# Gated convolution layer on one core: the sixth output product's weight difference on VectorE, eight block sums in a row, and additions moved between them

## The reference

```python
hn = rms_norm(x, norm_g)
a, b, gate = split(hn @ w_in, 3)              # w_in 1024 x 3072
u = a * sigmoid(b)
u = causal_depthwise_conv(u, conv_w, 31 taps) + conv_b
u = silu(layer_norm(u, ln_g, ln_b)) * silu(gate)
y = x + u @ w_out                             # w_out 1024 x 1024
```

## Time and profile before

| | |
|---|---|
| median of three executions | 354.58 us (354.42 to 354.72) |
| the profiled execution's own time | 354.64 us |
| its span in the profile | 352.8 us |
| PE busy | 348.5 us, 99% of the span |
| DVE busy | 322.4 us, 91% |
| POOL busy | 267.0 us, 76% |
| ACT busy | 232.0 us, 66% |
| DMA over the span | 123 GB/s on average |

### The profile page before, as it was taken

One profiled execution on the slowest core, in us unless ns is written; L12 is line 12 of the kernel. 1 busy time (PEld: TensorE's weight loads), 2 busy tenths in 40 slices (PEclk: granted clock), 3 DMA queues, 4 the chain that ended last, 5 costly groups with the idle time before them and its releaser, 6 DMA issues.

```text
span 352.8 us, 4758 instructions
## 1 busy us (share of the span) xinstructions
PE 348.5 (99%) x1564; PEld 289.6 (82%) x1564; DVE 322.4 (91%) x516; ACT 232.0 (66%) x334; POOL 267.0 (76%) x192
## 2 busy tenths in 40 slices
PE   8999999999999999999999999999999999999996
PEld 8888888888888888888888888888888888878785
DVE  5679799999999999989999998998599999999972
ACT  6889685667936870998669777975784872443400
POOL 0119999999999999789999999895596551359240
PEclk9999999999999999999999999999999999999999
DMA  8995111201410321404110410441643498047152
GB/s 265 411 412 212 39 59 59 88 34 61 118 61 16 88 78 59 119 2 119 59 60 3 119 59 15 107 119 61 215 143 120 130 394 313 0 151 224 45 208 90
DMA packets 30520, 43.51 MB, mean 123 GB/s; under 512 B 18336, under 2 KB 18848, under 8 KB 30496
## 3 DMA queue, kind: packets, MB, share of 16 engines
q1 hardware_dynamic: 30352, 43.21, 36.5%
q10 hardware_dynamic: 144, 0.00, 0.0%
HBM read 34.82 MB, written 4.19 MB: 111 GB/s over the span
## 4 chain that ended last, share of the span: by engine, by line
PE 92%; DVE 5%; issue 1%; ACT 0%; DVEq 0%; ACTq 0%
PE mm L634 68%; PE acc L710 9%; PE mm L651 6%; PE mm L710 6%; DVE sgate L1254 2%; DVE nat L1266 2%; DVE x_lo L1234 1%; PE acc L756 1%; PE acc L691 1%; PE acc L701 1%; PE acc L628 0%; ACT x_hi L948 0%; PE acc L622 0%; PE acc L624 0%; DVE ones L1069 0%
## 5 line engine op out<-in xcount | busy, mean ns | idle before, releaser
L634 PE MATMUL mm<-x_hi,w_hi 128*128 128x512 f32 x352 | 137.4, 390 | 0.0
L634 PE MATMUL mm<-x_hi,w_lo 128*128 128x512 f32 x352 | 137.0, 389 | 0.0
L634 PE MATMUL mm<-x_lo,w_hi 128*128 128x512 f32 x352 | 137.0, 389 | 0.0
L1178 DVE SCALAR_TENSOR_TENSOR acc<-u,chan,acc 128x512 f32<-128x512 f32 x157 | 110.5, 748 | 0.1
L1484 POOL TENSOR_TENSOR pconv<-pconv,prod 128x512 f32<-128x512 f32 x60 | 78.4, 1349 | 1.3 <-ACT prod L865 1.3
L634 PEld LDWEIGHTS mm<-x_hi,w_lo 128*128 128x128 f32 x352 | 66.1, 188 | 13.8
L634 PEld LDWEIGHTS mm<-x_lo,w_hi 128*128 128x128 f32 x352 | 66.1, 188 | 13.6
L634 PEld LDWEIGHTS mm<-x_hi,w_hi 128*128 128x128 f32 x352 | 66.1, 188 | 13.4
L1178 DVE SCALAR_TENSOR_TENSOR acc<-u,w_sum,acc 128x512 f32<-128x512 f32 x90 | 67.2, 747 | 2.5 <-ACT acc L847 2.3
L865 ACT ACTIVATE prod<-u,chan 128x512 f32<-128x512 f32 x69 | 47.9, 716 | 19.9 <-POOL pconv L1484 18.5
L1428 POOL TENSOR_TENSOR w_lo<-raw,w_hi 128x1024 fp32r<-128x1024 f32 (+1 forms) x21 | 50.3, 2395 | 8.7 <-ACT w_hi L814 8.6
(11 more groups left out here) (109 smaller groups left out, 527.6 us busy)
## 6 DMA issues: line engine op xcount, KB each, us to landing
raw<-w_in SPq DMA_DIRECT2D x22, 512.0 KB, 3.3
nat<-x_t SPq DMA_DIRECT2D x16, 256.0 KB, 5.4
sgate<-x SPq DMA_DIRECT2D x8, 512.0 KB, 10.2
raw<-w_out SPq DMA_DIRECT2D x8, 512.0 KB, 3.3
nat<-x SPq DMA_DIRECT2D x8, 512.0 KB, 7.7
y<-nat SPq DMA_DIRECT2D x15, 256.0 KB, 2.2
raw_late<-w_out SPq DMA_DIRECT2D x4, 512.0 KB, 4.3
sig<-w_out SPq DMA_DIRECT2D x4, 512.0 KB, 4.1
```

Source lines behind the costliest of these rows:

```text
L634: ins = nc.tensor.matmul(bank(("unit", m, h)), w[:, m % 3, k, :], xx[:, k, half(h)], start=(k == 0 and i == 0), stop=(k == KC - 1 and i == 2))
L1178: ins = nc.vector.scalar_tensor_tensor(dst, chain_in(j, chain, k), tap(j, chain, k), chain_bank(j, chain), ALU.mult, ALU.add)
```

## The change

The weight difference of b = 5 goes from POOL to DVE (`less_11`), and with it the semaphore that ACT and SP wait for. On DVE the sums of 5 and of 4 now stand in a row with no additions to the output between them, and additions that stood before and between them are spread behind. POOL's low halves of b = 4 wait for the last of the sums of 4, where they waited for the last of 5; its low halves of b = 5 wait for the last low part of v of b = 5 (6 x 4 of them), where the difference waited for the last of b = 4 (5 x 4).

```diff
-         ("12-11", 5, 0), ("12-11", 5, 1), ("lo", 5, 0), ("lo", 5, 1), ("lo", 6, 0), ("lo", 6, 1)]
+         ("lo", 5, 0), ("lo", 5, 1), ("lo", 6, 0), ("lo", 6, 1)]
-W_BY_VECTOR = {("+11", 4, 0): 1, ("+11", 4, 1): 2, ("lo", 3, 0): 3, ("lo", 3, 1): 4}
+W_BY_VECTOR = {("+11", 4, 0): 1, ("+11", 4, 1): 2, ("lo", 3, 0): 3, ("lo", 3, 1): 4, ("12-11", 5, 0): 5, ("12-11", 5, 1): 6}
-W_PAUSES = {("22-12", 2, 0): CK, ("lo", 2, 0): 2 * CK, ("21-", 3, 0): 4 * CK, ("12-11", 5, 0): 5 * CK, ("lo", 6, 0): 7 * CK}
+W_PAUSES = {("22-12", 2, 0): CK, ("lo", 2, 0): 2 * CK, ("21-", 3, 0): 4 * CK, ("lo", 5, 0): 6 * CK, ("lo", 6, 0): 7 * CK}
...
             for i in range(2):
-                sp.wait_ge(wb_done, W_OP["12-11", 5, i])
+                sp.wait_ge(wb_late, W_BY_VECTOR["12-11", 5, i])
                 load_w_out("a", i, 1, 1)
...
-                elif b == 4:
-                    act.wait_ge(wb_late, W_BY_VECTOR["+11", 4, i])
+                elif b in (4, 5):
+                    act.wait_ge(wb_late, W_BY_VECTOR[{4: "+11", 5: "12-11"}[b], b, i])
...
+            def less_11(i):
+
+                dve.wait_ge(wo_in[1][i], 64)
+                dve.wait_ge(wo_in[0][i], 48)
+                nc.vector.tensor_tensor(w_source(5, i), w_source(5, i), w_raw("a", i), ALU.subtract).then_inc(wb_late, 1)
...
             posts(2, (0,))
             for i in range(2):
                 finish_wb_lo(3, i)
-            posts(2, (1,))
+            posts(2, (1, 2))
             for k in range(CK):
                 sum_v(5, k)
-            posts(2, (2, 3))
             for k in range(CK):
                 sum_v(4, k)
+            posts(2, (3,))
+            posts(3, (0, 1))
             for k in range(CK):
                 split_v(4, k)
-            posts(3)
+            for i in range(2):
+                less_11(i)
+            for k in range(CK):
+                split_v(5, k)
+            posts(3, (2, 3))
             posts(4, (0, 1))
-            for k in range(CK):
-                split_v(5, k)
             for k in range(CK):
                 sum_v(6, k)
...
                 if op == ("lo", 4, 0):
-                    pool.wait_ge(vsum_ready, vsum_count(5, CK - 1))
+                    pool.wait_ge(vsum_ready, vsum_count(4, CK - 1))
```

More of the change, by code:

```diff
@@ L873, in split_w_out @@
                     act.wait_ge(wo_in[0][i], 16 if b == 1 else 64)
-                elif b == 4:
-                    act.wait_ge(wb_late, W_BY_VECTOR["+11", 4, i])
+                elif b in (4, 5):
+                    act.wait_ge(wb_late, W_BY_VECTOR[{4: "+11", 5: "12-11"}[b], b, i])
                 else:
-                    act.wait_ge(wb_done, W_OP[{2: "22-12", 3: "21-", 5: "12-11"}[b], b, i])
+                    act.wait_ge(wb_done, W_OP[{2: "22-12", 3: "21-"}[b], b, i])
                 if b == 3:
@@ L1370, in _ @@
                 finish_wb_lo(3, i)
-            posts(2, (1,))
+            posts(2, (1, 2))
             for k in range(CK):
                 sum_v(5, k)
-            posts(2, (2, 3))
             for k in range(CK):
                 sum_v(4, k)
+            posts(2, (3,))
+            posts(3, (0, 1))
             for k in range(CK):
                 split_v(4, k)
-            posts(3)
-            posts(4, (0, 1))
+            for i in range(2):
+                less_11(i)
             for k in range(CK):
                 split_v(5, k)
+            posts(3, (2, 3))
+            posts(4, (0, 1))
             for k in range(CK):
@@ L1448, in w_out_op @@
                     ins = nc.gpsimd.tensor_tensor(source, source, w_raw("b", i), ALU.subtract)
-                elif what == "21-":
+                else:
                     pool.wait_ge(spare_in[i], 16)
                     pool.wait_ge(wb_late, W_BY_VECTOR["+11", 4, i])
[L1452 to L1455, removed]
                     ins = nc.gpsimd.tensor_tensor(source, source, w_raw("a", i), ALU.subtract)
```

## The result

The changed kernel takes 355.26 us (median of 18 executions, 355.0 to 356.07); the kernel before, now also over 18, takes 354.82 (354.31 to 355.37). The ratio is 1.0014, 95% interval 1.0007 to 1.0020: 0.5 us slower by the ratio, between 0.25 and 0.7 us, and 0.44 us between the two medians. That is within the 0.2% that I called no change, and above the 355.0 us at which my range ended. The median of the kernel before stands 0.24 us above the three executions from which I had started.

What follows compares the result with a forecast made beforehand. PE, busy for 99% of the span, bounds the kernel; its breaks offered 1.10 us. Product 4's loss drops out and product 6 moves from 338.85 to 338.92: 354.58 + 0.07 = 354.65 us, range 354.1 to 355.0.

Steps and rivals of the forecast that it cites:

- The sums end free of POOL: On DVE, the eight sums of 5 and 4 run with no long one, done at 311.37, 4.0 us earlier.
- The splits of 4: On DVE, the first two splits for product 4 collide with POOL's low halves, taking 1.3 and 2.9 us.
- The gap at k = 1 of product 4: PE waits 0.62 us three matmuls into product 4, losing 0.81 us with what follows, where it was 0.24.
- VectorE waits for a DMA before its second difference: Before `less_11(1)`, DVE idles for about 1.2 us near 319.5 until the load of block 11 lands at 320.6.
- the second break: PE waits at k = 2 of product 5 for POOL's second low half: gap 0.21 us, plus 0.11 to 0.19 behind.
- its load is issued at 316.71 and takes 3.9 us: The load for `less_11(1)` lands at 320.6, with 3.9 us taken from the same load issued at 313.7.
- POOL's end to PE's start: Delay from a low part's end to the PE matmul waiting for it, put at 0.07 us.
- What is lost behind this gap: Further PE loss after the product 5 gap: 0.11 to 0.19 us, taken as 0.15 in the sum.
- The bound of 4.25 us at 355.0: If the load for `less_11(1)` takes 4.25 us to land, the kernel takes 355.0 us.
- B: Rival, chance 0.08: DVE's new wait for block 11's load decides from 3.7 us; from 4.6 us, over 0.71 us slower.

Runs made afterwards that it cites:

- e4: The kernel before with only product 5's weight difference moved to VectorE, behind the splits of product 4; ratio 0.9977 to the kernel before.
- e1: The changed kernel with block 11 for VectorE's difference loaded early into the spare buffer; ratio 0.9991 to the kernel before.
- e2: The changed kernel with the four stores of part 11 issued ahead of the second load of block 11; 358.55 us, ratio 1.0097 to the kernel before.
- e3: The changed kernel with the four stores of part 11 issued only after the loads that follow the weight difference; ratio 0.9995 to the kernel before.
- e6: The kernel before with only the eight sums in a row, moved additions and POOL's later wait, the difference staying on POOL; ratio 1.0027 to the kernel before.
- e5: The changed kernel with POOL's low halves of product 4 freed from waiting for the sums, and additions reordered; 353.91 us, ratio 0.9975 to the kernel before.

## Why the prediction was wrong, step by step

**Right: the mechanism and the place of every break.** The sums end free of POOL (7 x 0.60 and the last 0.68 make the 4.89 us). The splits of 4 were to take 1.3 and 2.9 us and take 1.33 and 2.89. The gap at k = 1 of product 4 was to be 0.62 us and is 317.48 - 316.87 = 0.61, with 0.77 us lost by its bank 2 (322.40 less 310.75 + 10.88) against 0.81. VectorE waits for a DMA before its second difference, and the second break stands at k = 2 of product 5, ended by POOL. The rule of the Trainium skill on the two engines (SBUF — State Buffer, "Who interferes with whom") is borne out by all further profiles: additions with an operand in PSUM are undisturbed (4.86 us for eight in e4, most of them beside POOL), operations with two operands in SBUF are not.

**Wrong: the size of the second break.** The step is "its load is issued at 316.71 and takes 3.9 us". It took 4.13, 0.23 us more, and e1, e2 and e3 show that this term goes into the end one for one or, removed, gives the break back. POOL's end to PE's start took 0.15 us (329.60 to 329.75), where I had put 0.07. What is lost behind this gap was 0.06 us less than I took. Together product 6 is 0.24 us later than forecast against product 3: 28.61 us against 338.92 - 310.55 = 28.37. With 0.07 us forecast, that is the 0.31 us that the profile shows.

**Wrong: the bounds.** I took 3.9 us from one row because it was the same load with the same neighbours. Five profiles with these neighbours have 3.9 to 4.2; mine was the lowest. The bound of 4.25 us at 355.0 was right in kind, but I laid it on 354.58, a median of three that 18 executions put at 354.82, and added nothing for that. On that base the same forecast is 354.89, and its upper bound 355.24; the measured 355.26 is still just above.

The miss of 0.61 us (355.26 less 354.65) is thus made of three parts: 0.24 us of base, 0.24 us in the stretch (0.23 of it the landing), and 0.13 us by which the medians lie further apart than the two stretches do (0.44 against 0.31). The last part lies within the interval; whether the landing is longer still in other executions was not measured. That the time stayed within what I called no change is owed to the slack of 0.2%: the interval of the ratio leaves out 1, and the sum left the change at 0.07 us.

**Of the rivals,** B named the mechanism that decided, DVE's new wait for the load, and gave the point from which it costs (3.7 us); at 4.1 us it costs what it said. I gave it 0.08 and only for long landings, while my own forecast already stood on it. The two halves should have been priced apart: the difference on VectorE gains 0.8 us (e4), the sums in a row with POOL's later start lose 0.6 to 1.3 us (e6). They also don't add up: in the stretch the halves make -0.80 and +0.57 us, together -0.23, and the whole change +0.31. What is left, 0.54 us, is close to the 0.64 us lost at the second break of the changed kernel (339.36 - 322.40, less 72 matmuls or 16.32 us). Only together do they make VectorE wait for a late load: in e4 the load is there in time, and in e6 no VectorE operation waits for it.

One correction to the description of the kernel before, on which nothing here rests: the POOL line of the weight difference is L1448 for b = 2 and L1452 for b = 3; L1456 is that of b = 5 alone.

## What to carry over

When two engines exclude each other, moving one engine's work later protects the operations beside which it stood and hits those behind; look for the stretch in which the partner does work that does not collide (here the additions from PSUM) and put it there, or let the two collide where the result isn't wanted yet (the sums in e5). Before an engine is made to wait, follow what its output frees: here a 3 us later low half made a load 3 us later that a different engine then waited for. And a term that decides the end should have its range from all rows like it, not from the one most like it.

## What the runs showed of the hardware

- Four stores of 256 KB that SP issues 0.4 us after a load of 512 KB slow that load: 3.9 to 4.2 us to landing in five profiles against 3.3 (e3) and 3.4 (e1) without them. Issued ahead, they make it 5.7 us (e2) and hold its issue back by 1.9 us.
- POOL and DVE took turns in all ten cases in which two low halves of POOL in a row met DVE operations with two operands in SBUF (two cases each in the kernel before and e6, one in each other profile): exactly one DVE operation came between POOL's two, each of the two DVE operations hit ended 0.54 to 0.56 us after a POOL operation, and POOL's second took 2.85 to 2.87 us against 2.40.
